# Feed-forward of a float32 two-block network on one core: output tiles as seven half-size block products, weight-quarter sums on GpSimd

## The reference

```python
def swiglu_ffn(x, w_in, w_out):
    gate, up = jnp.split(x @ w_in, 2, axis=-1)
    return (jax.nn.silu(gate) * up) @ w_out

x = x + 0.5 * swiglu_ffn(rmsnorm(x, norm_g), ffn_w_in, ffn_w_out)   # four times
```

## Time and profile before

| | us |
|---|---|
| median of 3 runs | 2587.79 |
| lowest and highest run | 2587.04, 2589.40 |
| span of the profiled execution, first to last instruction | 2585.3 |
| PE busy in it | 2552.6 |
| DVE busy | 1904.1 |
| ACT busy | 1264.0 |
| POOL busy | 191.5 |

### The profile page before, as it was taken

The page is one execution under the profiler, slowest core; times in us unless marked ns, Lnnn a source line. Parts: engine busy times, 40 slices in busy tenths (PEclk is TensorE's granted clock), DMA queues, the critical chain, the costliest instruction groups (busy, mean ns, idle before and its releaser), DMA issues.

```text
span 2585.3 us, 43699 instructions
## 1 busy us (share of the span) xinstructions
PE 2552.6 (99%) x17223; PEld 2171.8 (84%) x17223; DVE 1904.1 (74%) x3109; ACT 1264.0 (49%) x2140; POOL 191.5 (7%) x248
## 2 busy tenths in 40 slices
PE   9999999999999989999999999999999999999999
PEld 7787878887777768999988999989999864889998
DVE  5765655686666678877769777688777698897775
ACT  5544445456665654444454444454444413444444
POOL 1110101013000010000020000010000421100000
PEclk9999999999999999999999999999999999999999
DMA  4222222122222212333322332223323472322232
GB/s 137 84 82 67 82 67 92 40 82 102 81 81 73 73 50 82 107 114 107 99 99 82 115 99 98 99 82 105 108 98 99 127 180 75 98 98 99 98 100 81
DMA packets 171883, 241.78 MB, mean 94 GB/s; under 512 B 6545, under 2 KB 149403, under 8 KB 171443
## 3 DMA queue, kind: packets, MB, share of 16 engines
q1 hardware_dynamic: 164755, 216.27, 25.7%
q0 software_dynamic: 6368, 21.79, 3.0%
q10 hardware_dynamic: 576, 1.16, 0.1%
HBM read 233.54 MB, written 5.58 MB: 92 GB/s over the span
## 4 chain that ended last, share of the span: by engine, by line
PE 88%; DVE 6%; ACT 2%; issue 2%; DMA 1%; POOL 0%; SPq 0%; POOLq 0%; DVEq 0%; ACTq 0%
PE ps L2000 8%; PE ps L2002 8%; PE ps L2001 8%; PE ps L440 5%; PE ps L442 5%; PE ps L441 5%; PE ps L2020 5%; PE ps L2021 5%; PE ps L2022 5%; PE ps L858 5%; PE ps L860 4%; PE ps L859 4%; PE ps L2748 1%; DMA w_raw<-in_ffn_w_out_dram 1%; DVE probs L1814 1%
## 5 line engine op out<-in xcount | busy, mean ns | idle before, releaser
L858 PE MATMUL ps<-h_hi,w_hi 128*128 128x512 f32 x608 | 255.2, 420 | 2.5 <-DVE w_lo L417 1.3
L2020 PE MATMUL ps<-a_hi,w_hi 128*128 128x512 f32 x640 | 250.2, 391 | 4.6 <-DVE a_lo L2315 4.6
L2122 ACT ACTIVATE wg<-w_raw 128x512 fp32r<-128x512 f32 x256 | 153.7, 624 | 197.7 <-PE ps L2002 98.0
L2021 PE MATMUL ps<-a_lo,w_hi 128*128 128x512 f32 x640 | 249.8, 390 | 0.0
L2022 PE MATMUL ps<-a_hi,w_lo 128*128 128x512 f32 x640 | 249.5, 390 | 0.0
L860 PE MATMUL ps<-h_hi,w_lo 128*128 128x512 f32 x608 | 237.9, 391 | 0.0
L859 PE MATMUL ps<-h_lo,w_hi 128*128 128x512 f32 x608 | 237.8, 391 | 0.0
L2000 PE MATMUL ps<-mix_late,wg 128*128 128x256 f32 x832 | 235.2, 283 | 0.1
L2002 PE MATMUL ps<-mix_late,wg 128*128 128x256 f32 x832 | 234.7, 282 | 0.0
L2001 PE MATMUL ps<-mix_late,wg 128*128 128x256 f32 x832 | 234.6, 282 | 0.0
L417 DVE TENSOR_TENSOR w_lo<-w_raw,w_hi 128x2048 fp32r<-128x2048 f32 x90 | 206.1, 2290 | 29.4 <-ACT w_hi L412 29.4
(11 more groups left out here) (463 smaller groups left out, 6614.4 us busy)
## 6 DMA issues: line engine op xcount, KB each, us to landing
w_raw<-in_ffn_w_in_dram SPq DMA_DIRECT2D x88, 1024.0 KB, 5.1
w_raw<-in_ffn_w_out_dram SPq DMA_DIRECT2D x44, 1024.0 KB, 4.9
w_raw<-in_a_w_in_dram SPq DMA_DIRECT2D x24, 1024.0 KB, 5.4
w_raw<-in_b_w_in_dram SPq DMA_DIRECT2D x16, 1024.0 KB, 5.4
w_raw<-in_conv_w_pw_dram SPq DMA_DIRECT2D x12, 1024.0 KB, 5.9
shifted<-glu_scratch POOLq DMA_DIRECT2D x32, 264.0 KB, 7.5
w_raw<-in_a_w_out_dram SPq DMA_DIRECT2D x8, 1024.0 KB, 4.9
w_raw<-in_b_w_out_dram SPq DMA_DIRECT2D x8, 1024.0 KB, 4.9
```

Of the source, the lines that this page charges most:

```text
L858: nc.tensor.matmul(dst, wh[:, w], h_hi[:, k], start=k == 0, stop=False)
L2020: nc.tensor.matmul(dst, wh[:, w], a_hi[:, buf, k], start=h == 0 and k == 0, stop=False, skip_group_check=h == 1)
L2021: nc.tensor.matmul(dst, wh[:, w], a_lo[:, buf, k], start=False, stop=False, skip_group_check=h == 1)
```

## The change

Three of the five pairs, 1 to 3, get their output tiles by seven block products as well. In these pairs the output tile's quarters go through `quarter_sum`, `quarter_high` and `quarter_low` like the others. The hidden tile is cut in halves both ways, and DVE makes its differences (`hid_add`), ACT and DVE its high and low parts (`hid_high`, `hid_low`). PE's `pe_out_mix` adds the products of both steps in a PSUM bank, and DVE adds each finished product to xT, twice where it belongs to two parts of the output: 14 adds of 2 x 256 elements (`add_mixed`). All weight-quarter sums, those of gate and up tiles too, move from DVE's list to a new list of POOL (`gp_ff`). The ring gets two more slots in `w_hi` and `w_lo` for pairs 1 to 3, and slots are given out by the order in which PE frees them. A second hidden tile lies in `n_rstd` and `hid_even`. The lists of ACT and DVE are written anew (`act_steps`, `dve_steps`, and `act_last_steps`, `dve_last_steps` for pair 4).

```diff
+MIXED_PAIRS = (1, 2, 3)
+def mixed_tile(u, s):
+    return (s - 1) // 2 in MIXED_PAIRS if u == "o" else s >= PLAIN
+            hid_even = sb("hid_even", [P, T], into=s)
-        RING = 10
+        RING, RING_EXTRA = 10, 2
+        def out_bank(x, q):
+            return 4 + q if x in (1, 6, 7, 4) else 6 + q
+        HID_PART = {1: (0, 0), 5: (0, HT), 6: (1, 0), 7: (1, HT), 2: (2, 0), 3: (2, HT), 4: (3, 0)}
+        BANK_READ = {6: 1, 3: 5, 7: 6, 2: 3, 4: 7}
+        def pe_out_mix(pe, f, r, x, q, *hs):
+            for h in hs:
+                s, (k, o) = 2 * r + 1 + h, HID_PART[x]
+                pe.wait_ge(mix_lo, quarters_before(f, s, "o", x) + 1)
+                pe.wait_ge(hid_lo, hid_items_before(f, s, k) + 1)
+                if h == 0 and x in BANK_READ:
+                    pe.wait_ge(out_mix_added, out_groups_before(f, r, BANK_READ[x], q) + 1)
...
+                wh, wl = mix_slot(f, s, "o", x)
+                xh, xl = (part[:, o:o + HT] for part in hid_item(f, s, k))
+                for u in range(2):
+                    first = h == 0 and u == 0 and x in (1, 5, 2)
+                    dst, n = ps[:, out_bank(x, q), u * HT:u * HT + HT], 2 * q + u
+                    nc.tensor.matmul(dst, wh[:, n], xh, start=first, stop=False, skip_group_check=not first)
+                    nc.tensor.matmul(dst, wh[:, n], xl, start=False, stop=False, skip_group_check=not first)
+                    ins = nc.tensor.matmul(dst, wl[:, n], xh, start=False, stop=True, skip_group_check=not first)
...
+                if r in MIXED_PAIRS:
+                    for x in (1, 5):
+                        pe_out_mix(pe, f, r, x, 0, 0)
+                        pe_out_mix(pe, f, r, x, 1, 0)
+                    pe_mix(pe, f, b, "u", 4)
+                    for x in (1, 5):
+                        pe_out_mix(pe, f, r, x, 0, 1)
+                        pe_out_mix(pe, f, r, x, 1, 1)
+                    for x in (6, 3, 7, 2):
+                        pe_out_mix(pe, f, r, x, 0, 0, 1)
+                        pe_out_mix(pe, f, r, x, 1, 0, 1)
+                    continue
...
+        def hid_add(dve, f, s, k):
+            if k == 1:
+                out, a, b = hid_part(s, 0, 1), hid_part(s, 0, 1), hid_part(s, 0, 0)
+            elif k == 2:
+                out, a, b = t2, hid_part(s, 1, 1), hid_part(s, 0, 1)
+            elif k == 3:
+                out, a, b = t3, t2, hid_part(s, 0, 0)
+            else:
+                out, a, b = hid_part(s, 1, 0), hid_part(s, 1, 0), t2
+            nc.vector.tensor_tensor(out, a, b, ALU.subtract).then_inc(hid_sum, 1)
+        def hid_low(dve, f, s, k):
+            dve.wait_ge(hid_hi, hid_items_before(f, s, k) + 1)
+            nc.vector.tensor_tensor(lo, src, hi.bitcast(F32), ALU.subtract).then_inc(hid_lo, 1)
+        def add_mixed(dve, f, r, x, *qs):
+                src = ps[:, out_bank(x, q)].rearrange("p (u n) -> p u n", n=HT)
+                nc.vector.scalar_tensor_tensor(dst, src, 0.5, dst, ALU.mult, ALU.add).then_inc(out_mix_added, 1)
...
-        def quarter_sum(dve, f, s, u, *xs):
+        def quarter_sum(pool, f, s, u, *xs):
-            tt, t, i = nc.vector.tensor_tensor, step_tile(f, s, u), mixed_before(f, s, u)
+            tt, t, i = nc.gpsimd.tensor_tensor, step_tile(f, s, u), tile_before(f, s, u)
...
+        def gp_ff(pool, f, m):
+            pool.wait_ge(bcast_ready, SPREAD.index(m) + 1)
+            quarter_sum(pool, f, 2, "g", 5, 6, 7, 3)
+            quarter_sum(pool, f, 2, "u", 5, 6, 7, 3)
+            quarter_sum(pool, f, 3, "g", 5, 6, 7)
+            quarter_sum(pool, f, 3, "u", 5)
+            quarter_sum(pool, f, 3, "g", 3)
+            quarter_sum(pool, f, 3, "u", 7, 6, 3)
+            for r in MIXED_PAIRS:
+                a, b, c = 2 * r + 1, 2 * r + 2, 2 * r + 3
+                quarter_sum(pool, f, b, "g", 5, 6, 7, 3)
+                quarter_sum(pool, f, b, "u", 5, 6, 7, 3)
+                quarter_sum(pool, f, a, "o", 5, 6, 7, 3)
+                quarter_sum(pool, f, b, "o", 5, 6, 7, 3)
+                quarter_sum(pool, f, c, "g", 5, 6, 7)
+                quarter_sum(pool, f, c, "u", 5)
+                quarter_sum(pool, f, c, "g", 3)
+                quarter_sum(pool, f, c, "u", 7, 6, 3)
+            quarter_sum(pool, f, FF_STEPS - 1, "g", 5, 6, 7, 3)
+            quarter_sum(pool, f, FF_STEPS - 1, "u", 5, 6, 7, 3)
...
         def dve_steps(dve, f, r):
-            a, b = 2 * r + 1, 2 * r + 2
-            add_pair(dve, f, r - 1, 5)
-            quarter_sum(dve, f, b, "g", 5)
+            a, b, c = 2 * r + 1, 2 * r + 2, 2 * r + 3
+            join(dve, f, a, "g", "c11")
+            if r == 1:
+                add_pair(dve, f, 0, 6, 7)
+            quarter_low(dve, f, a, "u", 6, 2)
+            join(dve, f, a, "g", "c12")
+            join(dve, f, a, "g", "c22")
+            quarter_low(dve, f, a, "u", 3, 7, 4)
...
+            quarter_low(dve, f, b, "o", 6)
+            hid_add(dve, f, b, 3)
+            add_mixed(dve, f, r, 1, 0)
+            quarter_low(dve, f, b, "o", 2)
+            hid_low(dve, f, b, 1)
+            add_mixed(dve, f, r, 1, 1)
+            hidden(dve, f, b, "h21")
+            add_mixed(dve, f, r, 5, 0, 1)
+            hid_low(dve, f, b, 2)
+            quarter_low(dve, f, b, "o", 3)
+            add_mixed(dve, f, r, 6, 0)
...
```

More of the change, by code:

```diff
@@ L2248, in act_ff @@
             quarter_high(act, f, 3, "u", 1, 5, 6)
[L2249 removed]
+            for r in MIXED_PAIRS:
                 act_steps(act, f, r)
+            act_last_steps(act, f)
         def round_after(act, f):
[L2254 removed]
+            act.wait_ge(pair_half, (FF_PAIRS - len(MIXED_PAIRS)) * (f + 1))
             round_tile(act, end_of(f) + 1)
@@ L2422, in dve_steps @@
-            join(dve, f, a, "g", "c12")
-            quarter_low(dve, f, b, "g", 1)
+            a, b, c = 2 * r + 1, 2 * r + 2, 2 * r + 3
+            join(dve, f, a, "g", "c11")
[5 more added lines that the diff above has]
+            quarter_low(dve, f, a, "u", 3, 7, 4)
+            quarter_low(dve, f, b, "g", 1, 5, 6, 2)
+            join(dve, f, a, "u", "c11")
@@ new lines, in dve_steps @@
+            join(dve, f, a, "u", "c12")
+            hidden(dve, f, a, "h0")
+            hid_add(dve, f, a, 1)
+            join(dve, f, a, "u", "c22")
+            quarter_low(dve, f, b, "g", 3)
+            hidden(dve, f, a, "h22")
+            quarter_low(dve, f, b, "g", 7)
+            hid_low(dve, f, a, 0)
+            quarter_low(dve, f, b, "g", 4)
+            hid_add(dve, f, a, 2)
+            quarter_low(dve, f, b, "u", 1)
+            hidden(dve, f, a, "h21")
+            quarter_low(dve, f, b, "u", 5)
@@ new lines, in dve_steps @@
+            hid_add(dve, f, a, 3)
+            quarter_low(dve, f, b, "u", 6)
+            hid_low(dve, f, a, 2)
+            join(dve, f, b, "g", "c11")
+            quarter_low(dve, f, b, "u", 2)
+            hid_low(dve, f, a, 1)
+            join(dve, f, b, "g", "c12")
+            hid_add(dve, f, a, 4)
+            join(dve, f, b, "g", "c22")
+            quarter_low(dve, f, b, "u", 3, 7, 4)
+            quarter_low(dve, f, a, "o", 1, 5, 6, 2)
+            join(dve, f, b, "u", "c11")
+            join(dve, f, b, "u", "c12")
@@ new lines, in dve_steps @@
+            hidden(dve, f, b, "h0")
+            quarter_low(dve, f, a, "o", 3)
+            hid_add(dve, f, b, 1)
+            quarter_low(dve, f, a, "o", 7)
+            join(dve, f, b, "u", "c22")
+            quarter_low(dve, f, a, "o", 4)
+            hid_low(dve, f, b, 0)
+            quarter_low(dve, f, b, "o", 1)
+            hidden(dve, f, b, "h22")
+            quarter_low(dve, f, b, "o", 5)
+            hid_add(dve, f, b, 2)
+            quarter_low(dve, f, b, "o", 6)
+            hid_add(dve, f, b, 3)
@@ new lines, in dve_steps @@
+            add_mixed(dve, f, r, 1, 0)
[7 more added lines that the diff above has]
+            add_mixed(dve, f, r, 6, 0)
+            quarter_low(dve, f, b, "o", 7)
+            add_mixed(dve, f, r, 6, 1)
+            add_mixed(dve, f, r, 3, 0)
+            quarter_low(dve, f, b, "o", 4)
@@ new lines, in dve_steps @@
+            add_mixed(dve, f, r, 3, 1)
+            quarter_low(dve, f, c, "g", 1)
+            hid_add(dve, f, b, 4)
+            quarter_low(dve, f, c, "g", 5)
+            add_mixed(dve, f, r, 7, 0)
+            hid_low(dve, f, a, 3)
+            hid_low(dve, f, b, 3)
+            add_mixed(dve, f, r, 7, 1)
+            quarter_low(dve, f, c, "g", 6)
+            add_mixed(dve, f, r, 2, 0)
+            quarter_low(dve, f, c, "g", 2)
+            add_mixed(dve, f, r, 2, 1)
+            add_mixed(dve, f, r, 4, 0)
@@ L2424, in dve_steps, with dve_last_steps @@
+            quarter_low(dve, f, c, "g", 3, 7)
+            add_mixed(dve, f, r, 4, 1)
+            quarter_low(dve, f, c, "g", 4)
+            quarter_low(dve, f, c, "u", 1, 5)
+        def dve_last_steps(dve, f):
+            a, b = FF_STEPS - 2, FF_STEPS - 1
+            join(dve, f, a, "g", "c11")
```

(8 more changed lines are left out.)

423 lines of the change are left out of this document (276 added, 147 removed).

## The result

The changed kernel takes 2703.57 us (median of 4 runs, 2702.28 to 2705.71) against 2587.51 us (median of 4 runs too; the 2587.79 above was of three of them): ratio 1.0448, interval 1.0433 to 1.0463, slower by 116 us. Forecast were 2632 us and a range from 2566 to 2698: the direction was right, the size too small by 72 us, and the result lies 6 us beyond the range. The profiled execution's span went from 2585.3 to 2702.8 us, by 117.5.

The account below looks back on a forecast made before the run. PE bounds the kernel before; DVE was to set the mixed pairs at 67 us. With lead -6 and start +2, each feed-forward gains 11.1 us, four 44.4; 2585.3 became 2629.7, plus 2.5 gives 2632 us, range 2566 to 2698.

Parts of the forecast that it names:

- PE's saving: Mixed pairs: 168 short matmuls replace 96 long ones in the output, 1.84 us less per pair, floor 60.1 us.
- DVE's own work: Mixed pair: VectorE's instructions without the sums come to 47.4 us, 2.6 us more than before.
- Price of a POOL sum: Mixed pairs: a GpSimd sum between two-SBUF-input DVE instructions costs DVE 1.05 us, 0.87 us on average.
- "3" sums: Mixed pair: six quarter-3 sums that DVE waits for, 2.1 us each with ACT's part, 3.8 us uncovered in all.
- T = 67 us: Length of a mixed pair, set by DVE: 47.4 + 18 x 0.87 + 3.8 = 67 us, over PE's 60.1.
- Lead: Mixed pairs: DVE starts ahead of PE, and 6 us of that is used up once per feed-forward, between 3 and 9.
- The last plain pair at nothing: Last, plain pair of each feed-forward: DVE has 49 us of work in 62, so sums on POOL cost nothing.
- Start: Start of each feed-forward: eight sums moved to POOL make it 2 us worse, bounds -1.3 and +5.
- (a): Rival: PE stays the bound in mixed pairs, a sum costs DVE under 0.5 us; 2566 us, chance 0.20.
- (b): Rival: PE's gain and DVE's loss cancel near the break-even of 63.3 us a mixed pair; 2588 us, chance 0.08.
- (c): Rival: port hold lasts the whole POOL instruction, 1.18 us a sum on average, mixed pairs 72.5; 2698 us, chance 0.12.

Follow-up runs that it names:

- e1: Changed kernel with every weight-quarter sum on POOL replaced by one constant write that reads nothing, same waits and signals; 2569.7 us, ratio 0.9927.
- e5: Changed kernel with all 96 sums per feed-forward back in DVE's list, POOL idle, mixed output kept; 2625.0 us, ratio 1.0147.
- e7: Changed kernel with the sums of steps 2 and 3 (start of each feed-forward) as eight small writes without reads; 2676.2 us, ratio 1.0341.
- e8: Changed kernel with the sums of steps 9 and 10 (last, plain pair) as eight small writes without reads; 2681.7 us, ratio 1.0354.
- e3: Kernel before with its 72 sums per feed-forward moved from DVE's list to POOL's, no mixed output; 2617.0 us, ratio 1.0111.
- e4: Changed kernel with one DVE instruction, join c22 of (b, u), moved earlier to straight behind join c12; 2702.6 us, ratio 1.0438.

## Why the prediction went wrong in size

- **PE's saving.** 1.84 us a pair forecast, floor 60.1; e1 has 60.4 us pairs, 1.6 less than before, and is 20 us (ratio 0.9927) under the kernel before in all. Right, a little large.
- **DVE's own work.** 47.4 us forecast, 49.0 busy in e1. The work is right, but the tails before gaps, which the prediction names for the pair of before, were left out of the mixed pair's sum: 1.6 us.
- **Price of a POOL sum.** 1.05 us between two-SBUF instructions, measured 1.04. 18 x 0.87 = 15.7 us of blocks a pair, measured 15.3. The exclusion read from a few POOL instructions between the feed-forwards carried over. That the totals agree is in part luck: the six "3" sums were taken as blocking nothing, and three of them in the second mixed pair do hold DVE up, as this one, with a difference that takes 0.42 us alone; so the other 18 cost somewhat less than 0.87.

```profile
1165.70 1.61 POOL L2611 TENSOR_TENSOR w_raw<-w_raw,n_rb 128x512 f32<-128x512 f32 x1 [6.58 <-DVE wg L2644]
1166.42 1.17 DVE L2543 TENSOR_TENSOR f_hid<-f_hid,n_sq 128x256 f32<-128x256 f32 x1
```

- **T = 67 us.** Measured 68.8 in the pair read here, 68.9 on the mean of all twelve. The 1.8 us of this pair are the 1.6 of tails and 0.6 of idle time, less 0.4 of blocks. I took DVE's idle time as 3.8 us behind the "3" sums. It is 4.4 us and lies elsewhere: 1.4 for ACT, but 2.6 at one add that waits for PE. My reading is that PE waits for DVE 3.2 us, its product comes late, and DVE then waits for it. That is argued, not shown: e1 has a wait of 3.1 us at the same add though PE never stands there. e5, without blocks, has 1.4 us of idle time. With T = 68.9, 1.9 us x 12 = 23 us of the 72.
- **Lead.** The step that failed most. I took 6 us per feed-forward off, 24 us. The first mixed pair is as long as the third, even with 3.0 us less of DVE's busy time in it (61.4, 64.3): DVE comes out of the start with nothing, and PE already waits for it there. The earlier trace rows had such a wait, of 1.3 us at most, in the start of each feed-forward. e7, where the start's sums do not read, leaves room for a lead of 2.5 us at most. 24 us of the 72. The 11 us by which a low preceded its product in the earlier trace rows came in the middle of a run of pairs in which DVE had slack, and I read them as a stock left at the start of the mixed pairs. That they were the depth of the ring is likely and was not tested.
- **The last plain pair at nothing.** Measured +4.0 us per feed-forward, 16 us. DVE is busy 46 of 63 us, so the average said it fits; e8 shows that the loss goes with its own sums, and the full pairs of e3 that one blocked low half in front of PE is enough. e3's own last pair, with sums on POOL under the old list, loses nothing, so the new list of this pair has a part in it. The mistake: I asked whether DVE had room, not which of its instructions PE waits for next.
- **Start.** +2 us forecast, +2.8, 7.4, 3.1 and 2.9 measured, 8 us of the 72. The second one holds two stretches of some 3.4 us at half clock, and the others none:

```profile
1421.48:1475.36 53.88, 49.00 (x290) 43.71 (x289) 40.59 (x47) 20.40 (x36) 20.08 (x12) 0.94 0.30 98
```

- **Rivals.** (a) is excluded by e1 against the changed kernel: a sum costs 0.64 us of DVE, over its 0.5, and the pair is 8.4 us longer. (b), about 2588, is excluded by the result. (c) came within 6 us of the time by luck, not by its way: the hold is not 1.29 us, and not all sums are interposed.

The four together, 23 + 24 + 16 + 8 = 71, are the 72 us between forecast and result, to rounding.

## What to carry to other kernels

Work moved to GpSimd that reads SBUF is not off VectorE: here a sum of 0.60 us came back as 0.64 on average and as 1.04 between two instructions with two inputs in SBUF. It hits whichever of these is next, also in stages where VectorE has slack. Before counting on an engine's lead or average room, look at the stage ahead of it (does the bound engine already wait there?) and at each instruction the bound engine needs at once. A write-only stand-in with the same waits is a cheap test of the port against the order.

## What the runs showed of the hardware

PE's granted clock fell behind a stall. Windows of the changed kernel: PE idle for 3.2 us, and 0.8 us behind it 3.4 us at 0.50 (1.2 GHz, where full speed is 2.4); the third row is the same in the next pair. In the start of the second feed-forward it fell behind waits of 1.8 and 2.4 us too:

```profile
1109.57:1112.79 3.22, 0.00 (x1) 0.04 (x1) 3.22 (x4) 2.61 (x5) 3.14 (x3) 1.00 0.00 0
1113.60:1117.00 3.40, 3.17 (x16) 2.88 (x15) 3.40 (x8) 0.00 (x0) 0.00 (x0) 0.50 0.52 157
1181.90:1185.30 3.40, 3.40 (x17) 3.26 (x17) 3.40 (x7) 0.00 (x0) 0.27 (x1) 0.50 0.33 110
```

Some 16 matmuls start in the 3.4 us, 0.21 us apart in place of 0.12, which costs about 1.5 us. In this kernel that lies on time DVE needs anyway: e4's pair has a mean clock of 0.95 in place of 0.98 and the same 68.76 us:

```profile
1138.33:1207.09 68.76, 63.38 (x507) 62.66 (x506) 64.27 (x91) 33.62 (x69) 35.82 (x25) 0.95 0.28 93
```
